# A two-block float32 forward pass: three products of the mixing and ple phases summed in one set of 256 PSUM columns

## The chip, the cores and the metric

One core of a Trainium2 chip runs the whole program. The metric is the device time of one execution in microseconds (us). Engines are called as the profile calls them: PE is TensorE, DVE VectorE, ACT ScalarE, POOL GpSimd and SP SyncE, whose queue issues the weight loads from HBM.

## What is computed

Two transformer-like blocks on one sequence of 256 positions with 2048 channels, all in float32. Each block projects its input, runs small mixers on the projections (a linear recurrence, pooling, short convolution and attention in the first; two kinds of attention in the second), sums their gated projections, and then runs a feed-forward part. The lines that matter here are the gated sums and the small product `e`:

```python
# first block: four branches of width 512
branches = jnp.einsum('bskw,kwd->bskd', ys, w_branch[l])
merged = jnp.sum(gates * branches, axis=2)
x = x + merged @ w_out[l]
# second block: two branches of width 512, and e from p of width 256
mix = (gate_a * ya + gate_b * yb) @ w_out[i]       # ya, yb: branch outputs @ w_branch_a, w_branch_b
e = p[i] @ w_ple_in[i]
h = h + jax.nn.sigmoid(h @ w_ple_gate[i]) * e
```

## The kernel before

Everything is kept transposed: 128 channels on the partitions, 256 positions (`S`) along the free dimension. Every large product runs as a stream of **units**. A unit makes 256 output channels (two tiles `t` of 128) by 256 positions. Its weights come in **pieces** of 512 KB: four k-tiles of 128 rows by 256 columns (two k-tiles in the phase `ple`). A phase (`plan()`, lines 120 to 158) is a list of units with one source of weights; most have 4 pieces in a unit (`ppu`), the four phases `mix_a0` to `mix_a3`, the two phases `mix_b0` and `mix_b1` and the phase `ple` have one. Each of these seven phases has 8 units.

To hold float32 accuracy, each operand is split into a high part (rounded to the format `fp32r`) and a low part (the rest). For activations, high and low stand side by side, 512 columns (`act_a`, `act_b`); for weights they are two buffers, `wh` and `wl`. A piece passes through a ring of four slots:

- SP loads it into `raw` (line 547) when DVE has split the piece four earlier.
- ACT makes `wh` (line 879) when the load has landed and PE has used the piece four earlier (`w_used`).
- DVE makes `wl = raw - wh` (line 1216).
- PE runs, for each k-tile and each t, two matmuls (lines 580 and 582): `wh` by the 512 columns [high | low], and `wl` by the 256 columns of high. So PSUM holds in columns 0:256 the sum wh·xh + wl·xh, and in columns 256:512 the sum wh·xl. A unit takes one of two PSUM buffers in turn, and a new unit waits until the unit two earlier has been summed (`summed`).

The **epilogue** of a unit adds the two halves: ACT copies columns 256:512 to `bcopy` (line 893), and DVE adds columns 0:256 to it (line 1241, or 1236 for `ple`, `w_out2` and `ffn_down0`). In the mixing phases a unit is one branch of one pair of output tiles. DVE multiplies its sum by the gate (line 1288 for the first branch, 1290 for the others), and POOL adds the later branches to the merged sum (line 1675). In `mix_a3` and `mix_b1` the finished sum also has to be split for the next phase: POOL's addition, then ACT's high part (line 932), then DVE's low part (line 1225).

Each engine runs its instructions strictly in the written order. In the mixing phases the order is that of `threaded`: DVE and ACT hold three pieces of lead (piece u+3 is prepared between the epilogue steps of unit u). At the end of such a phase the first pieces of the next phase (3 if it is a mixing phase, 4 otherwise) are prepared after the epilogue of unit 6 and ahead of that of unit 7. `ple` runs in the order of `fed` with one piece of lead, and its last units are interleaved with the normalisation before `ffn_up0` (`post_norm`, line 1605 on DVE).

## Time and profile before

| | us |
|---|---|
| median of 3 runs | 3088.48 (3086.43 to 3089.05) |
| the profiled execution, its own time | 3071.16 |
| its span, first to last instruction | 3069.3 |
| mean granted TensorE clock | 0.988 |

The span is what the rows below describe. Sections of the profile: busy time of each engine, the span in slices, the DMA queues, the chain that ended last, and groups of instructions by source line. Other views used are stretches of the span with the busy time of each engine, and timelines of one engine, in which a bracket gives the idle time ahead of an instruction and what ended it. Instructions of one engine overlap a little at their edges, so the distance of two starts is often less than the duration of the first.

### The profile page before, as it was taken

How to read it: one execution, taken by the hardware profiler on the slowest of the kernel's cores; microseconds unless marked ns; L12 is line 12 of the kernel's file. 1: busy time of each engine (PE TensorE's matmuls, PEld its weight loads, DVE VectorE, ACT ScalarE, POOL GpSimd, SP SyncE). 2: the span in 40 equal slices, each digit the busy share in tenths (PEclk: the TensorE clock that was granted, in tenths of full speed). 3: DMA queues.
4: the chain of work that ended last, by engine and by line, in shares of the span. 5: the costliest groups of instructions: out<-in, count | busy, mean ns of one | idle time of the engine just before them, and what ended most of it. 6: DMA issues, size and time to landing. Idle time of an engine off the chain costs nothing. (4 is left out here: it accounts for less than half of the span.)

```text
span 3069.3 us, 48743 instructions
## 1 busy us (share of the span) xinstructions
PE 2967.5 (97%) x16830; PEld 2571.2 (84%) x16830; DVE 1973.4 (64%) x2245; ACT 1551.1 (51%) x1953; POOL 257.8 (8%) x217
## 2 busy tenths in 40 slices
PE   7999999999999999999999998999799999999979
PEld 6788888888888888888888887878588888888867
DVE  6486676656665656556656655665777567657664
ACT  5485654454544444444544455444466455545544
POOL 3010011102101010000200000001300000010131
PEclk9999999999999999999999999999899999999989
DMA  7555557665666666665665544546366666565545
GB/s 215 158 165 165 165 167 217 181 178 171 192 192 192 189 188 191 190 187 180 197 191 172 170 148 141 185 151 190 107 187 185 186 190 189 187 185 185 173 134 165
DMA packets 544861, 544.78 MB, mean 177 GB/s; under 512 B 17032, under 2 KB 543880, under 8 KB 544752
## 3 DMA queue, kind: packets, MB, share of 16 engines
q1 hardware_dynamic: 543200, 539.42, 57.7%
q0 software_dynamic: 1552, 3.97, 0.4%
q8 instruction: 60, 0.98, 0.1%
q14 instruction: 49, 0.40, 0.0%
HBM read 541.23 MB, written 2.10 MB: 177 GB/s over the span
## 5 line engine op out<-in xcount | busy, mean ns | idle before, releaser
L1216 DVE TENSOR_TENSOR w_low<-raw,w_high 128x1024 fp32r<-128x1024 f32 x1024 | 1276.3, 1260 | 857.1 <-ACT w_high L879 852.6
L580 PE MATMUL ps_gemm<-act_a,w_high 128*128 128x512 f32 x4640 | 1643.1, 399 | 60.5 <-DVE w_low L1216 39.2
L879 ACT CAST w_high<-raw 128x1024 fp32r<-128x1024 f32 x1024 | 1056.6, 1045 | 961.7 <-PE ps_gemm L582 925.4
L582 PE MATMUL ps_gemm<-act_a,w_low 128*128 128x256 f32 x4640 | 1303.8, 281 | 0.0
L580 PE MATMUL ps_gemm<-act_b,w_high 128*128 128x512 f32 x3520 | 1240.6, 397 | 14.9 <-DVE w_low L1216 5.7
L580 PEld LDWEIGHTS ps_gemm<-act_a,w_high 128*128 128x128 f32 x4640 | 876.9, 189 | 276.6 <-issue 59.5
L582 PE MATMUL ps_gemm<-act_b,w_low 128*128 128x256 f32 x3520 | 986.9, 280 | 0.0
L582 PEld LDWEIGHTS ps_gemm<-act_a,w_low 128*128 128x128 f32 x4640 | 882.6, 190 | 0.2
L580 PEld LDWEIGHTS ps_gemm<-act_b,w_high 128*128 128x128 f32 x3520 | 663.3, 188 | 170.6 <-issue 10.6
L582 PEld LDWEIGHTS ps_gemm<-act_b,w_low 128*128 128x128 f32 x3520 | 667.8, 190 | 0.2
L893 ACT COPY bcopy<-ps_gemm 128x512 f32<-128x512 f32 x300 | 173.6, 579 | 88.1 <-PE ps_gemm L582 88.0
L1241 DVE TENSOR_TENSOR summ<-ps_gemm,bcopy 128x512 f32<-128x512 f32 x276 | 188.8, 684 | 28.1 <-ACT bcopy L893 27.3
L1689 POOL TENSOR_TENSOR proj<-proj,summ 128x512 f32 x32 | 41.4, 1292 | 1016.3 <-DVE summ L1241 1016.3
L1304 DVE SCALAR_TENSOR_TENSOR gates<-summ,params,gates 128x254 f32<-128x254 f32 (+1 forms) x176 | 77.3, 480 | 17.7 <-ACT gates L946 10.7
L1250 DVE TENSOR_TENSOR summ<-summ,rstd 128x512 f32<-128x512 f32 x124 | 85.8, 692 | 4.3
L1675 POOL TENSOR_TENSOR proj<-proj,summ 128x512 f32 x32 | 46.5, 1455 | 400.2 <-DVE summ L1290 400.2
L1657 POOL TENSOR_TENSOR sqacc<-sqacc,sqt 128x512 f32<-128x512 f32 x48 | 67.8, 1413 | 126.4 <-ACT sqt L964 114.3
L912 ACT CAST act_a<-summ 128x512 f32 (+1 forms) x32 | 19.9, 622 | 96.9 <-DVE summ L1263 96.9
L946 ACT ACTIVATE gates<-summ,params 128x256 f32<-128x256 f32 x88 | 48.2, 595 | 21.0 <-DVE summ L1250 19.0
L1257 DVE SCALAR_TENSOR_TENSOR act_b<-proj,params,act_b (+1 forms) x32 | 26.6, 873 | 49.8 <-ACT act_b L905 49.8
L899 ACT ACTIVATE gates<-summ 128x512 f32<-128x512 f32 (+1 forms) x40 | 25.3, 632 | 63.1 <-DVE summ L1250 63.0
L1225 DVE TENSOR_TENSOR act_a<-summ,act_a 128x512 f32 (+1 forms) x32 | 22.2, 693 | 32.5 <-ACT act_a L912 32.5
(239 smaller groups left out, 911.0 us busy)
## 6 DMA issues: line engine op xcount, KB each, us to landing
raw<-in_w_in SPq DMA_DIRECT2D x352, 512.0 KB, 4.2
raw<-in_w_up SPq DMA_DIRECT2D x176, 512.0 KB, 3.6
raw<-in_w_mlp_up SPq DMA_DIRECT2D x128, 512.0 KB, 3.9
raw<-in_w_mlp_down SPq DMA_DIRECT2D x128, 512.0 KB, 4.2
raw<-in_w_down SPq DMA_DIRECT2D x88, 512.0 KB, 4.4
raw<-in_w_out SPq DMA_DIRECT2D x64, 512.0 KB, 4.6
raw<-in_w_branch SPq DMA_DIRECT2D x32, 512.0 KB, 4.0
raw<-in_w_ple_gate SPq DMA_DIRECT2D x32, 512.0 KB, 4.4
```

The source lines that it names most:

```text
L580: nc.tensor.matmul(ps[:, g, t, :], wh[:, at, o:o + P], x, start=first, stop=False, skip_group_check=True)
L582: last = nc.tensor.matmul(ps[:, g, t, 0:S], wl[:, at, o:o + P], high(x), start=False, stop=final, skip_group_check=True)
L879: nc.scalar.copy(wh[:, at, 0:kn * S], raw[:, at, 0:kn * S]).then_inc(high_ready, 1)
L893: nc.scalar.copy(bcopy[:, g], ps[:, g, :, S:2 * S]).then_inc(b_copied, 1)
L946: last = nc.scalar.activation(G[:, 28 + 2 * j + t, :], summ[:, g, t], ACT.Identity, scale=pcol("conv_w2", c0 + t + 176), bias=pcol("conv_b ...
L1216: nc.vector.tensor_tensor(wl[:, at, 0:kn * S], raw[:, at, 0:kn * S], wh[:, at, 0:kn * S].bitcast(F32), ALU.subtract).then_inc(split_done, 1)
L1241: nc.vector.tensor_tensor(s2, A_half, bcopy[:, g], ALU.add).then_inc(summed, 1)
L1250: nc.vector.tensor_tensor(s2, s2, r2, ALU.mult).then_inc(scaled, 1)
L1304: last = nc.vector.scalar_tensor_tensor(out=y[:, t, sh:S], in0=summ[:, g, t, 0:S - sh], scalar=pcol("conv_w2", c0 + t + 88 * tap), in1=y[: ...
L1657: nc.gpsimd.tensor_tensor(sqacc[:], sqacc[:], sqt[:, g], ALU.add).then_inc(inc, 1)
L1675: nc.gpsimd.tensor_tensor(d, d, s2, ALU.add).then_inc(merged if split else epi_done, 1)
L1689: nc.gpsimd.tensor_tensor(d, d, s2, ALU.add).then_inc(epi_done, 1)
```

## The change

In the phases `mix_a0` to `mix_a3`, `mix_b0`, `mix_b1` and `ple` (the function `folded`), the 512-column matmul becomes two of 256 columns, `wh` by high and `wh` by low, and both go to PSUM columns 0:256, where `wl` by high goes too. PSUM then holds the full sum, and columns 256:512 are no longer used. ACT's epilogue returns at once (no copy). DVE waits for PE itself (`w_used`): in the mixing phases it multiplies PSUM by the gate in one instruction, in `ple` it copies PSUM to its place. For a first branch DVE now waits for the end of that multiplication and for the unit before, and then signals `epi_done` by hand. POOL waits for `summed` in place of `scaled`. Counters are adjusted for the units that have no copy. Of `ADDS`, the entries of the branch phases under `scaled` go. `source`, `over`, `threaded` and `fed` are unchanged.

```diff
@@ -113,6
+def folded(ph):
+    return ph.kind.startswith("branch") or ph.name == "ple"
...
+        copied += 0 if folded(x) else x.units
...
+def copied_no(ph, i, j):
+    return i * ph.U + (ph.copied0 + j)
...
@@ -577,8 +587,14 @@
                     final = s == ph.ppu - 1 and k == kn - 1
                     for t in range(2):
                         o = k * S + t * P
-                        nc.tensor.matmul(ps[:, g, t, :], wh[:, at, o:o + P], x,
-                                         start=first, stop=False, skip_group_check=True)
+                        if folded(ph):
+                            nc.tensor.matmul(ps[:, g, t, 0:S], wh[:, at, o:o + P], high(x),
+                                             start=first, stop=False, skip_group_check=True)
+                            nc.tensor.matmul(ps[:, g, t, 0:S], wh[:, at, o:o + P], x[:, S:2 * S],
+                                             start=False, stop=False, skip_group_check=True)
+                        else:
+                            nc.tensor.matmul(ps[:, g, t, :], wh[:, at, o:o + P], x,
+                                             start=first, stop=False, skip_group_check=True)
                         last = nc.tensor.matmul(ps[:, g, t, 0:S], wl[:, at, o:o + P], high(x),
                                                 start=False, stop=final, skip_group_check=True)
                 last.then_inc(w_used, 1)
@@ -888,6 +904,8 @@
 
             def epilogue(ph, i, j):
                 k, g, n = ph.kind, bank(ph, j), unit_no(ph, i, j)
+                if folded(ph):
+                    return
                 act.wait_ge(w_used, end_piece(ph, i, j))
                 act.wait_ge(summed, n + 1)
                 nc.scalar.copy(bcopy[:, g], ps[:, g, :, S:2 * S]).then_inc(b_copied, 1)
@@ -1229,10 +1247,19 @@
                 t0 = dst_tile(ph, i, j)
                 A_half = ps[:, g, :, 0:S]
                 s2 = summ[:, g]
-                dve.wait_ge(b_copied, n + 1)
+                if folded(ph):
+                    dve.wait_ge(w_used, end_piece(ph, i, j))
+                else:
+                    dve.wait_ge(b_copied, copied_no(ph, i, j) + 1)
                 dve.wait_ge(epi_done, n + 1)
+                if ph.name == "ple":
+                    nc.vector.tensor_copy(tiles(G, t0, 2), A_half).then_inc(summed, 1)
+                    dve.wait_ge(summed, n + 1 + 2)
+                    dve.wait_ge(epi_done, n + 2)
+                    dve.sem_inc(epi_done, 1)
+                    return
                 if k in ("mix", "store"):
-                    dst = tiles(G, t0, 2) if ph.name == "ple" else tiles(PJ, t0 + 16, 2)
+                    dst = tiles(PJ, t0 + 16, 2)
                     nc.vector.tensor_tensor(dst, A_half, bcopy[:, g], ALU.add).then_inc(summed, 1)
                     dve.wait_ge(summed, n + 1 + 2)
                     dve.wait_ge(epi_done, n + 2)
@@ -1281,13 +1308,17 @@
                 def gated():
                     nb = 4 if k.startswith("branch4") else 2
                     br = j % nb
+                    dve.wait_ge(w_used, end_piece(ph, i, j))
+                    dve.wait_ge(epi_done, n + 1)
+                    total = ps[:, g, :, 0:S]
                     gate = gate_tiles(ph, i * 2 + 4 * br) if nb == 4 else tiles(G, i * 4 + (12 + 8 * br + 2 * (j // 2)), 2)
-                    dve.wait_ge(summed, n + 1 + 2)
                     if br == 0:
+                        nc.vector.tensor_tensor(tiles(PJ, t0 + 16, 2), total, gate, ALU.mult).then_inc(summed, 1)
+                        dve.wait_ge(summed, n + 1 + 2)
                         dve.wait_ge(epi_done, n + 2)
-                        nc.vector.tensor_tensor(tiles(PJ, t0 + 16, 2), s2, gate, ALU.mult).then_inc(epi_done, 1)
+                        dve.sem_inc(epi_done, 1)
                     else:
-                        nc.vector.tensor_tensor(s2, s2, gate, ALU.mult).then_inc(scaled, 1)
+                        nc.vector.tensor_tensor(s2, total, gate, ALU.mult).then_inc(summed, 1)
                         if br == nb - 1 and k.endswith("s"):
                             dve.wait_ge(high_out, after("high_out", ph, i, j))
                             low(tiles(act_a if nb == 4 else act_b, t0, 2), tiles(PJ, t0 + 16, 2), epi_done)
@@ -1324,7 +1355,7 @@
                         low(tiles(act_b, t0, 2), G[:, 30:32, :], epi_done)
                 if k == "upconv":
                     return [total, taps, product, rest]
-                return [total, gated] if k.startswith("branch") else [total]
+                return [gated] if k.startswith("branch") else [total]
 
             def recip(n):
 
@@ -1667,7 +1698,7 @@
                 if k.startswith("branch"):
                     nb = 4 if k.startswith("branch4") else 2
                     if j % nb:
-                        pool.wait_ge(scaled, after("scaled", ph, i, j))
+                        pool.wait_ge(summed, n + 1 + 2)
                         pool.wait_ge(epi_done, n + 2)
                         d = tiles(PJ, t0 + 16, 2)
                         split = j % nb == nb - 1 and k.endswith("s")
```

## Rows read from the trace of the kernel before

**Rows 1.** Page, part 1: busy time of each engine, share of span, instructions.
```profile
PE 2967.5 (97%) x16830; PEld 2571.2 (84%) x16830; DVE 1973.4 (64%) x2245; ACT 1551.1 (51%) x1953; POOL 257.8 (8%) x217
```

**Rows 2.** Stretches mix_a0, mix_b1: length; busy PE, PEld, DVE, ACT, POOL; clock; DMA.
```profile
430.00:456.20 26.20, 25.02 (x140) 21.08 (x138) 23.64 (x25) 13.02 (x18) 7.18 (x5) 1.00 0.51 159
2044.00:2073.00 29.00, 22.66 (x110) 18.97 (x109) 21.22 (x27) 12.08 (x18) 3.86 (x3) 0.88 0.41 126
```

**Rows 3.** PE's timeline at full pace in mix_a0: start, duration, instruction.
```profile
437.86 0.40 PE L580 MATMUL ps_gemm<-act_b,w_high 128*128 128x512 f32 x1
438.10 0.28 PE L582 MATMUL ps_gemm<-act_b,w_low 128*128 128x256 f32 x1
438.21 0.40 PE L580 MATMUL ps_gemm<-act_b,w_high 128*128 128x512 f32 x1
...
439.98 0.40 PE L580 MATMUL ps_gemm<-act_b,w_high 128*128 128x512 f32 x1
```

**Rows 4.** PE's timeline at full pace in mlp_up0, the same columns.
```profile
849.81 0.39 PE L580 MATMUL ps_gemm<-act_b,w_high 128*128 128x512 f32 x1
...
851.89 0.39 PE L580 MATMUL ps_gemm<-act_b,w_high 128*128 128x512 f32 x1
```

**Rows 5.** PE's timeline: 18 transposes, each with its own weight load.
```profile
1723.28 2.17 PE L794 MATMUL ps_small<-proj 128*128 128x128 f32 x18
```

**Rows 6.** Groups by line: busy us, mean ns | idle before, releaser.
```profile
L582 PEld LDWEIGHTS ps_gemm<-act_b,w_low 128*128 128x128 f32 x3520 | 667.8, 190 | 0.2
L893 ACT COPY bcopy<-ps_gemm 128x512 f32<-128x512 f32 x300 | 173.6, 579 | 88.1 <-PE ps_gemm L582 88.0
L1675 POOL TENSOR_TENSOR proj<-proj,summ 128x512 f32 x32 | 46.5, 1455 | 400.2 <-DVE summ L1290 400.2
```

**Rows 7.** DVE's timeline in mix_a0 and at its end.
```profile
441.58 0.68 DVE L1241 TENSOR_TENSOR summ<-ps_gemm,bcopy 128x512 f32<-128x512 f32 x1
442.18 2.11 DVE L1216 TENSOR_TENSOR w_low<-raw,w_high 128x1024 fp32r<-128x1024 f32 x1
444.22 0.68 DVE L1290 TENSOR_TENSOR summ<-summ,gates 128x512 f32<-128x512 f32 x1
444.82 0.68 DVE L1241 TENSOR_TENSOR summ<-ps_gemm,bcopy 128x512 f32<-128x512 f32 x1
...
450.36 1.32 DVE L1290 TENSOR_TENSOR summ<-summ,gates 128x512 f32<-128x512 f32 x1
451.60 4.58 DVE L1216 TENSOR_TENSOR w_low<-raw,w_high 128x1024 fp32r<-128x1024 f32 x3
456.10 0.68 DVE L1241 TENSOR_TENSOR summ<-ps_gemm,bcopy 128x512 f32<-128x512 f32 x1
```

**Rows 8.** PE's timeline: stops at the edges of mix_a0 and mix_a2, in mix_a3, after mix_b0.
```profile
452.87 0.50 PE L580 MATMUL ps_gemm<-act_b,w_high 128*128 128x512 f32 x1 [0.93 <-DVE w_low L1216]
456.90 0.49 PE L580 MATMUL ps_gemm<-act_b,w_high 128*128 128x512 f32 x1 [0.96 <-DVE summ L1241]
592.32 0.50 PE L580 MATMUL ps_gemm<-act_a,w_high 128*128 128x512 f32 x1 [0.94 <-DVE w_low L1216]
704.37 0.49 PE L580 MATMUL ps_gemm<-act_b,w_high 128*128 128x512 f32 x1 [2.10 <-DVE summ L1241]
710.95 0.50 PE L580 MATMUL ps_gemm<-act_a,w_high 128*128 128x512 f32 x1 [0.76 <-DVE w_low L1216]
1945.30 0.50 PE L580 MATMUL ps_gemm<-act_b,w_high 128*128 128x512 f32 x1 [1.21 <-DVE w_low L1216]
```

**Rows 9.** DVE's timeline in mix_b1: the first and the last low part.
```profile
2049.34 0.69 DVE L1225 TENSOR_TENSOR act_b<-proj,act_b 128x512 fp32r<-128x512 f32 x1 [2.41 <-ACT act_b L932]
...
2075.24 0.69 DVE L1225 TENSOR_TENSOR act_b<-proj,act_b 128x512 fp32r<-128x512 f32 x1 [2.41 <-ACT act_b L932]
```

**Rows 10.** DVE's timeline in ple: two of its sums.
```profile
2167.34 0.69 DVE L1236 TENSOR_TENSOR gates<-ps_gemm,bcopy 128x512 f32<-128x512 f32 x1 [2.19 <-ACT bcopy L893]
...
2185.48 0.69 DVE L1236 TENSOR_TENSOR gates<-ps_gemm,bcopy 128x512 f32<-128x512 f32 x1 [0.64 <-ACT bcopy L893]
```

More of the change, by code:

```diff
@@ L98, in __init__ @@
         self.quarter, self.group, self.half = quarter, group, half
-        self.piece0 = self.unit0 = self.bodies = 0
+        self.piece0 = self.unit0 = self.bodies = self.copied0 = 0
         self.count0 = {}
 ADDS = {
-    "scaled": {"gate": [1, 1, 1, 1], "branch4": [0, 1, 1, 1], "branch4s": [0, 1, 1, 1], "branch2": [0, 1, 0, 1],
-               "branch2s": [0, 1, 0, 1], "up": [1, 1], "upconv": [1, 1], "final": [1, 1]},
+    "scaled": {"gate": [1, 1, 1, 1], "up": [1, 1], "upconv": [1, 1], "final": [1, 1]},
     "acted": {"up": [1, 1], "upconv": [1, 1], "final": [1, 1]},
@@ L147, in plan @@
     ph.append(Phase("final", 8, 2, 4, name="ple_gate"))
-    piece = unit = 0
+    piece = unit = copied = 0
     count = {k: 0 for k in ADDS}
@@ L151, in plan @@
         assert x.units % x.U == 0 and (x.U % 2 == 0 or x.units == 1) and (x.U * x.ppu) % RING == 0
-        x.piece0, x.unit0, x.bodies = piece, unit, x.units // x.U
+        x.piece0, x.unit0, x.bodies, x.copied0 = piece, unit, x.units // x.U, copied
         x.count0 = dict(count)
```

## The prediction

> **What bounds the kernel now.** I read part 1 of the page first. PE is busy for 97% of the span [rows 1], so for most of the run an instruction taken from ACT or DVE is worth nothing. Next I read the stretches of the phases that the change touches, for here PE does stop. In `mix_a0` it is busy 25.02 of 26.2 us, and DVE 23.64. In `mix_b1` PE is busy 22.66 of 29.0 us, and the clock that it was granted falls to 0.88 [rows 2]. Last I read the timelines, to see who ends the stops.
>
> At full pace one pair (512 and 256 columns) takes (439.98 - 437.86) / 6 = 0.353 us [rows 3]. A mixing unit has 8 pairs, 2.83 us. DVE in the same unit does a sum, a weight split and a gate: from 441.58 to 444.82 is 3.24 us [rows 7]. So in the mixing phases DVE is slower than PE by 0.41 us a unit. Its split takes 2.11 us here, against a mean of 1.53 for the three that start at 451.60. The difference is POOL's addition beside it, 1.46 us on average [rows 6, 7]. The three pieces of lead hide this inside a phase. It shows at the edges: PE stops before the first unit of the next phase, which waits for DVE's split, and before the second, which waits for DVE's sum of the old phase's last unit [rows 8]. That sum stands behind three splits, at 456.10 [rows 7].
>
> **What the change does to PE.** Each of the 6 x 64 mixing pairs gets one matmul and one weight load more, with the same number of columns. The trace has no two 256-column matmuls of this format in a row. The nearest row is the 256-column one between two others: its successor starts 0.11 us later (438.10 to 438.21), and in that time a full weight load was taken in [rows 3]. Three such steps are 0.33 to 0.35 us, against the pair's 0.353 now. Can loads follow at this rate? In 18 transposes in a row, each with a load of 128x128, the starts are (2.17 - 0.28) / 17 = 0.11 us apart [rows 5]. I therefore take the pair as unchanged. The bounds: three times 0.11 gains 0.02 us x 384 = 8 us; a load that can't be hidden costs 66 us (below).
>
> The Trainium skill, TensorE: Matmul & The Clock Gate, section LDWEIGHTS, gives a load as its columns divided by 1.2, 107 ns for 128; by that, three loads would fit the pair, and rows 3 and 5 agree. The Trainium skill, Perfetto Trace Analysis, Identifying the Most-Contended Engine, speaks against the change: it judges TensorE by the busy share of LDWEIGHTS. That share is 21.08 of 26.2 us in mix_a0 [rows 2], and with half as many loads again it would be 120%.
>
> **What it does to ACT.** 48 copies of 0.58 us go from the mixing phases and 8 from ple [rows 6]. ACT's busy time there is about half the stretch [rows 2], so the 32 us of work are worth nothing by themselves. What counts is that DVE no longer waits for the copy, and that casts no longer stand behind it. DMA issues hang on DVE's splits alone and move forward with them; no queue is blocked more than now.
>
> **What it does to DVE.** In a mixing unit two instructions of 0.68 us (0.60 from start to start, 444.22 to 444.82) become one [rows 7]. I price it at 0.68 too, since it reads one operand from PSUM and one from SBUF, as the sum does. A unit then takes 3.24 - 0.60 = 2.64 us, 0.19 less than PE. Added: a first-branch unit waits for its own end, priced at 0 to 0.25 us. Behind it on DVE stands the next split, which has three pieces of lead. One more thing helps: the gate that reads two SBUF tiles took 1.32 us beside POOL at 450.36; the sum from PSUM at 441.58 did not stretch [rows 7].
>
> The gains, edge by edge. A bracket's idle time understates a stop: the matmul ahead is drawn 0.28 us long, but its successor could start after 0.11, and the first matmul after a stop is 0.10 longer [rows 3, 8]. I add 0.26 to each.
>
> - mix_a0 to mix_a1: 0.93 and 0.96 idle, and the like of the first at the end of mix_a1: 3 x 1.2 = 3.6 us [rows 8]. After the change unit 6 is done on DVE 0.68 + 2.11 = 2.8 us after PE ends it, split of the next piece included, and PE's unit 7 takes 2.83. I leave 0.1 of each stop: gain 3.3.
> - mix_a2: 0.94 idle, gain 1.1 [rows 8].
> - mix_a3: 2.10 and 0.76 idle, 3.4 with the additions [rows 8]. The 2.10 come from the detour POOL, ACT, DVE (2.41 idle on DVE in its twin in mix_b1 [rows 9]). DVE reaches the detour one unit's wait earlier, as it is no longer late: gain 3.3. The stop ahead of the phase's third unit, where DVE is busy with the merged low parts, stays.
> - mix_b0: 1.21 idle, gain 1.5 [rows 8].
> - mix_b1: here four detours in eight units make DVE's own chain the bound, up to the last low part at 2075.24 [rows 9], on which the next phase's third piece waits. Each of 8 units loses one instruction, 0.60; after three detours only about 0.47 counts, as DVE then waits for ACT's cast. That is 4.4 us. The own-end waits of four first branches give back 0.25 each at most: 3.4 to 4.4, I take 4.0.
> - ple: DVE copies instead of summing, at the same 0.68. Only the waits for ACT shrink: 0.64 of the idle at 2185.48 and one copy's time, 0.58, at 2167.34 [rows 6, 10], and 0.58 more where ACT's cast no longer stands behind a copy: 1.8. What is late next is DVE in `post_norm`, unchanged.
>
> Sum: 3.3 + 1.1 + 3.3 + 1.5 + 4.0 + 1.8 = 15.0, and 1 of the 8 us that PE's pair could gain at best: 16 us. Against the profiled execution, 3071.2 - 16 = 3055 us; that execution is 17.3 us under the median, and I take the same gain from the median: 3088.5 - 16 = 3072.5 us.
>
> **The rivals.** *The weight load becomes PE's bound.* If loads don't overlap each other, a pair needs 3 x 0.190 = 0.57 us [rows 6], a unit 4.56 instead of 2.83: 48 x 1.73 = 83 us more, less the stops, which vanish: about 3155 us. It decides as soon as a load and a 256-column matmul need over 0.118 us. For it: the loads' share in rows 2, and that no three short steps in a row are in the trace. Against it: rows 5. In a mild form (10 ns for each added matmul) it costs 4 us and leaves 3076.
>
> *DVE stays the bound.* The margin of 0.19 us a unit is thin: if a wait or POOL's port takes 0.2 to 0.3 us a unit, the edges keep half their stops. Gain 16 - 1/2 x (3.3 + 1.1 + 3.3 + 1.5) = 11, less 1 to 2 in mix_b1: 3079 us.
>
> *PE's pace changes with the form or the code's place.* The same pair takes 0.347 us in mlp_up0 (2.08 / 6) [rows 4] and 0.353 in mix_a0, and the rows don't say why. If two 256-column matmuls beat the 512-column one, the lower bound above holds: 3065 us. If a later phase of 256 pairs passes from one pace to the other, that is 1.7 us either way for each.
>
> *The gain is given back later,* because the chain through `post_norm` or the loads holds the end: the phases behind are bound by PE, which starts them earlier, so I see no place for it. Time within 0.2%.
>
> **How the numbers follow.** Forecast 3072.5: 0.58. DVE stays the bound, 3079: 0.15. A faster pair, 3065: 0.12. Given back or nothing gained: 0.06. The load as a bound: 0.09. The range takes in the forecast with its errors, the faster pair and the half gain, and leaves out the last two: 3063 to 3082. A measurement of this kernel can tell about 0.2%, 6 us, from no change. Faster by more: 0.84; within: 0.07; slower: 0.09.
>
> **What would show it.** In the changed kernel's trace the pair of rows 3 becomes three starts about 0.115 us apart; three at 0.15 or more refute the first step. DVE's cycle in mix_a0 falls from 3.24 us to PE's 2.83, with idle time ahead of the gate that PE ends. The stops of rows 8 are under 0.3 us, apart from the kept one. The four low parts of mix_b1 span 22 us instead of 25.9 [rows 9]. In ple the sums wait for PE. Wrong would be: a PE that is busy throughout mix_a0 with a longer stretch (loads), or the stops of rows 8 unchanged (DVE).

## The result and the profile after

| | before | after |
|---|---|---|
| median (range) of 6 runs each, one comparison | 3088.8 (3086.4 to 3101.7) us | 3061.4 (3055.6 to 3068.3) us |
| profiled execution (its span) | 3071.2 (3069.3) us | 3064.2 (3062.4) us |
| all runs of this study: number, median, mean with its error | 85, 3077.2, 3077.8 ± 0.9 us | 23, 3060.9, 3062.7 ± 1.4 us |

The ratio of the first comparison is 0.9913 [0.989, 0.9936]: 27 us less, where I had forecast 16, and 3061.4 lies below the range (3063 to 3082). But the two profiled executions differ by only 6.9 us in span, and over all runs of the study the medians differ by 16.3 us, the means by 15.1. So there are three figures for one change, and the explanation must give all three. Below, a gain given beside a ratio is worked out from the ratio.

The page of after, part 1, and the groups that answer to [rows 1] and [rows 6]:

```profile
PE 2972.5 (97%) x17246; PEld 2590.4 (85%) x17246; DVE 1933.2 (63%) x2197; ACT 1523.7 (50%) x1897; POOL 265.4 (9%) x217
```
```profile
L911 ACT COPY bcopy<-ps_gemm 128x512 f32<-128x512 f32 x244 | 140.9, 577 | 35.7 <-PE ps_gemm L598 35.7
...
L1706 POOL TENSOR_TENSOR proj<-proj,summ 128x512 f32 x32 | 55.5, 1733 | 378.0 <-DVE summ L1321 377.9
...
L591 PE MATMUL ps_gemm<-act_b,w_high 128*128 128x256 f32 x256 | 72.7, 284 | 2.5 <-DVE proj L1316 2.3
```

PE has 416 matmuls more: 384 in the mixing phases and 32 in ple, which my count of the pairs had left out. ACT's copies fell from 300 to 244, DVE has 48 instructions fewer, and one thing rose that I had not looked at: POOL's addition, from 1455 to 1733 ns.

The stretches mix_a0 and mix_b1 of after (length; busy PE, PEld, DVE, ACT, POOL; clock; DMA), against [rows 2]:

```profile
433.50:457.00 23.50, 23.50 (x198) 23.50 (x197) 15.46 (x16) 9.88 (x10) 9.38 (x5) 1.00 0.51 161
2031.00:2064.00 33.00, 28.81 (x221) 27.35 (x220) 22.22 (x31) 14.59 (x23) 4.55 (x4) 1.00 0.45 134
```

The stretch of mix_a0 ends here ahead of the stop at the phase's edge, and that of [rows 2] behind it. The stretch of before that leaves the edge out in the same way is this one:

```profile
429.20:451.80 22.60, 22.60 (x128) 19.30 (x127) 19.38 (x22) 12.27 (x17) 5.16 (x4) 1.00 0.54 170
```

Inside the phase PE is busy throughout in both kernels, and DVE's share fell from 86% to 66%; what became of the edge is shown below. In mix_b1 PE still stops, but the granted clock is 1.00 over the whole stretch, not 0.88.

PE's timeline in mix_a0 of after, against [rows 3]:

```profile
436.94 0.28 PE L591 MATMUL ps_gemm<-act_b,w_high 128*128 128x256 f32 x1
437.06 0.28 PE L593 MATMUL ps_gemm<-act_b,w_high 128*128 128x256 f32 x1
437.18 0.28 PE L598 MATMUL ps_gemm<-act_b,w_low 128*128 128x256 f32 x1
437.30 0.28 PE L591 MATMUL ps_gemm<-act_b,w_high 128*128 128x256 f32 x1
```

Three steps of 0.12 make 0.36 us, where the pair took 0.353 or 0.347. Now DVE's and POOL's timelines in mix_a0 of after, against [rows 7], and last POOL's in before beside the split of 442.18:

```profile
442.90 0.69 DVE L1321 TENSOR_TENSOR summ<-ps_gemm,gates 128x512 f32<-128x512 f32 x1 [1.06 <-PE ps_gemm L598]
443.51 1.22 DVE L1234 TENSOR_TENSOR w_low<-raw,w_high 128x1024 fp32r<-128x1024 f32 x1
445.78 0.69 DVE L1316 TENSOR_TENSOR proj<-ps_gemm,gates 128x512 f32<-128x512 f32 x1 [1.06 <-PE ps_gemm L598]
```
```profile
443.80 2.07 POOL L1706 TENSOR_TENSOR proj<-proj,summ 128x512 f32 x1 [0.81 <-DVE summ L1321]
```
```profile
441.93 1.28 POOL L1675 TENSOR_TENSOR proj<-proj,summ 128x512 f32 x1 [1.95 <-DVE summ L1290]
```

The cycle is 445.78 - 442.90 = 2.88 us, which is PE's eight triples (8 x 0.36). DVE waits 1.06 us of it for PE. The split takes 1.22 us, not 2.11, and this time it is POOL's addition that is long. It begins at 443.80, behind the split's begin at 443.51. In before it began at 441.93, ahead of the split at 442.18, took 1.28 us, and the split was the long one. The order changed because POOL is released by the gate: in before a sum of 0.60 us stood between the gate and the split, and in after the split follows the gate at once. The Trainium skill, SBUF — State Buffer, SBUF: two separate sides, has VectorE with two SBUF inputs and GpSimd share one pair of ports, which whoever starts first keeps for its whole instruction; the two traces agree (2.11 us in one order, 2.07 on POOL in the other). Nobody waits for POOL here, so the exchange is free.

The stops of PE in after, against [rows 8], the first at the edge to mix_a1, the second the kept one in mix_a3, the others in mix_b1:

```profile
457.46 0.38 PE L591 MATMUL ps_gemm<-act_b,w_high 128*128 128x256 f32 x1 [0.20 <-DVE summ L1321]
...
689.84 0.38 PE L591 MATMUL ps_gemm<-act_b,w_high 128*128 128x256 f32 x1 [2.27 <-DVE proj L1316]
...
2037.71 0.39 PE L591 MATMUL ps_gemm<-act_a,w_high 128*128 128x256 f32 x1 [0.92 <-DVE proj L1316]
...
2044.55 0.38 PE L591 MATMUL ps_gemm<-act_a,w_high 128*128 128x256 f32 x1 [0.83 <-DVE proj L1316]
...
2051.39 0.38 PE L591 MATMUL ps_gemm<-act_a,w_high 128*128 128x256 f32 x1 [0.82 <-DVE proj L1316]
```

And DVE in mix_b1 of after, its first and last low part and the wait for its own end, against [rows 9]:

```profile
2041.99 0.69 DVE L1243 TENSOR_TENSOR act_b<-proj,act_b 128x512 fp32r<-128x512 f32 x1 [2.40 <-ACT act_b L950]
2044.60 1.23 DVE L1234 TENSOR_TENSOR w_low<-raw,w_high 128x1024 fp32r<-128x1024 f32 x1 [0.18 <-DVEq L1319]
...
2065.37 0.69 DVE L1243 TENSOR_TENSOR act_b<-proj,act_b 128x512 fp32r<-128x512 f32 x1 [2.39 <-ACT act_b L950]
```

The four low parts span 23.38 us (25.90 before, 22 forecast), and the detour over ACT (2.40) is untouched.

### The profile page after: what moved, and what is told of

Its sections match the earlier page's. It is cut to its first block and busy times, and to the rows that moved or that the text cites. A ratio compares the mean times of both kernels' runs of the same rounds, so it can differ in the third digit from the quotient of the medians.

```text
span 3062.4 us, 49424 instructions
## 1 busy us (share of the span) xinstructions
PE 2972.5 (97%) x17246; PEld 2590.4 (85%) x17246; DVE 1933.2 (63%) x2197; ACT 1523.7 (50%) x1897; POOL 265.4 (9%) x217
## 5 line engine op out<-in xcount | busy, mean ns | idle before, releaser
L596 PE MATMUL ps_gemm<-act_a,w_high 128*128 128x512 f32 x4480 | 1584.8, 399 | 43.7 <-DVE w_low L1234 25.8
L596 PE MATMUL ps_gemm<-act_b,w_high 128*128 128x512 f32 x3264 | 1150.2, 398 | 6.3 <-DVE act_b L1243 4.7
L596 PEld LDWEIGHTS ps_gemm<-act_a,w_high 128*128 128x128 f32 x4480 | 846.4, 189 | 252.0 <-issue 41.4
L596 PEld LDWEIGHTS ps_gemm<-act_b,w_high 128*128 128x128 f32 x3264 | 614.2, 188 | 153.6 <-issue 6.0
L1268 DVE TENSOR_TENSOR summ<-ps_gemm,bcopy 128x512 f32<-128x512 f32 x228 | 156.0, 684 | 22.0 <-ACT bcopy L911 21.4
L911 ACT COPY bcopy<-ps_gemm 128x512 f32<-128x512 f32 x244 | 140.9, 577 | 35.7 <-PE ps_gemm L598 35.7
L1720 POOL TENSOR_TENSOR proj<-proj,summ 128x512 f32 x32 | 41.4, 1293 | 1016.2 <-DVE summ L1268 1016.2
L1706 POOL TENSOR_TENSOR proj<-proj,summ 128x512 f32 x32 | 55.5, 1733 | 378.0 <-DVE summ L1321 377.9
L591 PE MATMUL ps_gemm<-act_b,w_high 128*128 128x256 f32 x256 | 72.7, 284 | 2.5 <-DVE proj L1316 2.3
L593 PE MATMUL ps_gemm<-act_b,w_high 128*128 128x256 f32 x256 | 72.4, 283 | 0.0
L591 PE MATMUL ps_gemm<-act_a,w_high 128*128 128x256 f32 x160 | 48.4, 302 | 10.6 <-DVE w_low L1234 8.0
```

Of the source, the lines that this page charges most:

```text
L591: nc.tensor.matmul(ps[:, g, t, 0:S], wh[:, at, o:o + P], high(x), start=first, stop=False, skip_group_check=True)
L593: nc.tensor.matmul(ps[:, g, t, 0:S], wh[:, at, o:o + P], x[:, S:2 * S], start=False, stop=False, skip_group_check=True)
L596: nc.tensor.matmul(ps[:, g, t, :], wh[:, at, o:o + P], x, start=first, stop=False, skip_group_check=True)
L911: nc.scalar.copy(bcopy[:, g], ps[:, g, :, S:2 * S]).then_inc(b_copied, 1)
L1268: nc.vector.tensor_tensor(s2, A_half, bcopy[:, g], ALU.add).then_inc(summed, 1)
L1706: nc.gpsimd.tensor_tensor(d, d, s2, ALU.add).then_inc(merged if split else epi_done, 1)
```

## How the spans were taken apart

From the starts of the matmuls of a trace I took two sums. *Stops*: what a start-to-start time has beyond the step usual there (0.116 us behind 256 columns, 0.233 behind 512), waits and stretches at the lower clock alike, where it is over 0.13 or 0.25. *Pace*: for every 512 + 256 pair that ran unbroken, what it took beyond 0.3467 us, the shorter of the two paces of [rows 3, 4]. The rest is span less both. How the small matmuls between the phases are counted moves the sum of stops as a whole: over all matmuls it is 142.7 us in before and 124.4 in after, over those of the large products alone 196.2 and 177.8. The difference stays 18.3 or 18.4, and only differences are used here.

| execution | span | stops | pace | rest |
|---|---|---|---|---|
| before | 3069.3 | 192.3 | 19.3 | 2857.7 |
| before again (e1_before) | 3084.9 | 192.6 | 34.6 | 2857.7 |
| after | 3062.4 | 174.0 | 25.0 | 2863.4 |
| after again (e2_after) | 3059.1 | 173.7 | 22.1 | 2863.3 |
| after, third (e12_after5) | 3064.4 | 174.6 | 25.7 | 2864.1 |

The stops fell by 18.5 us, alike in every execution. The rest rose by about 6 us: these are the 416 triples, which are counted in no pace (416 x (0.360 - 0.3467) = 5.5 us). And the pace has nothing to do with the change: it differs by 15 us between two executions of the very same kernel, which is their difference in span (15.6). The experiments below take these three apart.

## Experiments

**The kernel before, again.** No edit, three rounds.

> The kernel before, once more, for a second profile. Between the first two profiles the spans differ by 6.9 us, the medians of the runs by 27 us. Theory A (pace): whole phases run at 0.347 or 0.353 us a pair of matmuls, and which one is drawn anew in each execution; then this profile has the same PE stops as the first (within 1 us in all phases together), but other phases at the slow pace, and its span lies by up to 20 us above 3069.3, 1.7 us for each phase of 256 pairs that changed. Theory B (stops): the executions differ in PE stops; then a longer span comes with more stop time and the paces are as before. The time is that of the kernel before, ratio 1.000 within 0.002.

Measured: 3073.1 us (3064.1 to 3088.2) against 3074.5 of its partner, ratio 1.000 [0.9979, 1.0022]. The first comparison's 3088.5 is at the upper end of what this kernel shows. Its profiled execution was 15.6 us longer than the first one of before, and almost all of it lies in one stretch, from the first pair behind the row sums of mlp_up0 to the row sums behind the last mlp phase. PE's timeline, first of before, then of before again:

```profile
813.91 0.59 PE L580 MATMUL ps_gemm<-act_b,w_high 128*128 128x512 f32 x1
...
1524.08 0.59 PE L615 MATMUL ps_small<-sqacc,common 128*128 128x256 f32 x2
```
```profile
815.71 0.58 PE L580 MATMUL ps_gemm<-act_b,w_high 128*128 128x512 f32 x1
...
849.81 0.40 PE L580 MATMUL ps_gemm<-act_b,w_high 128*128 128x512 f32 x1
...
851.93 0.40 PE L580 MATMUL ps_gemm<-act_b,w_high 128*128 128x512 f32 x1
...
1539.52 0.59 PE L615 MATMUL ps_small<-sqacc,common 128*128 128x256 f32 x2
```

The same work, without a stop in either, takes 710.17 us in one and 723.81 in the other. [Rows 4] have six pairs in 2.08 us (0.347 each); here the same six, at the same place of the program, take 2.12 (0.353). So the pace doesn't belong to a line or a form: the same instructions have one or the other.

**The kernel after, again.** No edit.

> The changed kernel, once more, for a second profile. Theory A: the PE stops in the changed phases are as in its first profile (about 20 us fewer than before in all), the folded group of three matmuls takes 0.360 us in every mixing phase again, and the span differs from 3062.4 only by phases at the other pace. Theory B: the stops differ. Ratio to the kernel before 0.991 within 0.003.

Measured: 3060.8 us (3054.5 to 3077.3), ratio 0.996 [0.9937, 0.9983], a gain of 12 us. Five rounds more (e12_after5) gave 3063.4 us (3050.9 to 3076.6), 0.9939 [0.9907, 0.9971], a gain of 19. The 27 us of the first comparison did not come back.

> The changed kernel against the kernel before in more rounds, as the draws of the pace spread single runs over 25 us. So far the ratios are 0.991 and 0.996. By the profiles' parts: PE stops 192.4 - 173.9 = 18.6 us fewer; 384 groups at 0.360 against a mean of 0.350 us cost 3.8; so about 15 us less, a ratio of 0.9952, within 0.002. If the first comparison's 27 us were real, 0.991.

**Only the split of the matmul.** In before, the 512-column matmul of the mixing phases and ple as two of 256, into the columns as of old; copy and sum stay.

```diff
-nc.tensor.matmul(ps[:, g, t, :], wh[...], x, start=first, ...)
+nc.tensor.matmul(ps[:, g, t, 0:S], wh[...], high(x), start=first, ...)
+nc.tensor.matmul(ps[:, g, t, S:2 * S], wh[...], x[:, S:2 * S], start=False, ...)
...
```

> The matmul alone: in the mixing phases and ple the 512-column matmul is two of 256 columns, but into the old columns, and ACT's copy and DVE's sum stay. Stops theory: the three matmuls take 0.360 us against 0.353, so PE needs 2.88 us a unit, and DVE's cycle of 3.24 us still bounds the mixing phases; most of the 0.06 us a unit is hidden, and the time is 0 to 3 us above the kernel before. Weight-load rival of the prediction in its mild form: 4 us or more above. If the gain of the change came from the form of the matmuls or from the place of the code, this kernel would be faster than before by 5 us or more.

Measured: 3076.3 us, ratio 1.0015 [0.9998, 1.0033]: +4.6 us, inside its noise (its mean is 0.5 ± 2.6 us above that of all runs of before). Its stops sum to 187.6 us, 5 less than before's, though nothing was taken from DVE. DVE's timeline shows why:

```profile
446.77 0.68 DVE L1247 TENSOR_TENSOR summ<-ps_gemm,bcopy 128x512 f32<-128x512 f32 x1
447.40 2.07 DVE L1222 TENSOR_TENSOR w_low<-raw,w_high 128x1024 fp32r<-128x1024 f32 x1
...
450.00 0.68 DVE L1247 TENSOR_TENSOR summ<-ps_gemm,bcopy 128x512 f32<-128x512 f32 x1
```

DVE's cycle is 3.23 us as before, and PE's is 2.88 instead of 2.8. PE catches up with DVE more slowly and stops for less. So a slower PE gives its own price back, as shorter stops: by the traces 4.7 us of stops against the 4 to 5.5 us that 416 triples cost.

**The split in every phase,** to see the price of the form by itself.

```diff
-if ph.kind.startswith("branch") or ph.name == "ple":
+if True:
```

> The kernel before with the 512-column matmul made two of 256 columns, into the same columns as before, in every phase. This prices the form alone on some 8000 groups, where PE is the bound. If three matmuls always take 0.360 us, as in the mixing phases of the changed kernel, against a pair that is drawn at 0.347 or 0.353: 8000 x 0.010 = 80 us more, at most 8160 x 0.0133 = 109, so a median of 3140 to 3175. If the 0.360 belongs to short phases only and the three also have a faster pace of 3 x 0.1167 = 0.350: 0 to 30 us more. If a load were the bound: several hundred us more.

Measured: 3156.0 us (3153.6 to 3158.6), ratio 1.0245 [1.0198, 1.0293]. Against the 3077.2 of all runs of before that is 78.8 us on 24990 - 16830 = 8160 triples, 0.0097 us each. PE's timeline and part 1 of its page:

```profile
1000.00 0.28 PE L581 MATMUL ps_gemm<-act_a,w_high 128*128 128x256 f32 x1
1000.12 0.28 PE L583 MATMUL ps_gemm<-act_a,w_high 128*128 128x256 f32 x1
1000.24 0.28 PE L588 MATMUL ps_gemm<-act_a,w_low 128*128 128x256 f32 x1
1000.36 0.28 PE L581 MATMUL ps_gemm<-act_a,w_high 128*128 128x256 f32 x1
```
```profile
PE 3057.0 (97%) x24990; PEld 3026.7 (96%) x24990; DVE 1968.9 (62%) x2245; ACT 1549.9 (49%) x1953; POOL 257.9 (8%) x217
```

The steps are 0.120 again. There is no fast variant of the triple: its four runs lie within 5 us, where the ten of before in e1_before spread over 24. Four runs are few, but that is what one expects if the two paces exist only for the pair. For the change it means 416 x 0.0097 = 4.0 us of cost.

The Trainium skill, Perfetto Trace Analysis, Identifying the Most-Contended Engine, asks for the busy share of LDWEIGHTS (beside the share of the peak rate that the matmuls reach). It went to 100% in mix_a0 of after and to 96% here, and the time did rise, so the page pointed the right way; the size it could not tell, since these records overlap (0.19 us long, 0.12 apart).

**DVE keeps its second instruction.** In after, DVE copies the sum from PSUM and then gates it; ACT's copy stays out.

```diff
+def copied():
+    dve.wait_ge(w_used, end_piece(ph, i, j))
+    ...
+    nc.vector.tensor_copy(s2, ps[:, g, :, 0:S]).then_inc(summed, 1)
 def gated():
-    total = ps[:, g, :, 0:S]
+    total = s2
...
-return [gated] if k.startswith("branch") else [total]
+return [copied, gated] if k.startswith("branch") else [total]
```

> The changed kernel, but in the mixing phases DVE keeps two instructions: it copies PSUM to summ and then multiplies by the gate. ACT's copy is gone and the three products are folded. If DVE's instruction is what the gain comes from: DVE's cycle in mix_a0 is again about 3.2 us, the stops at the ends of the mixing phases return, and of some 27 us only 4 to 8 us remain (ple, and DVE's waits for ACT's copy in mix_a3 and mix_b1). If the removed ACT copy is what counts: 20 us or more remain.

Measured: 3070.8 us, ratio 0.9984 [0.9964, 1.0004], a gain of 4.9 us. DVE's timeline in its mix_a0, and the stop of PE at the phase's end:

```profile
441.59 0.69 DVE L1312 COPY summ<-ps_gemm 128x512 f32<-128x512 f32 x1
442.20 2.08 DVE L1235 TENSOR_TENSOR w_low<-raw,w_high 128x1024 fp32r<-128x1024 f32 x1
444.20 0.68 DVE L1324 TENSOR_TENSOR summ<-summ,gates 128x512 f32<-128x512 f32 x1
444.80 0.68 DVE L1312 COPY summ<-ps_gemm 128x512 f32<-128x512 f32 x1
...
456.89 0.38 PE L592 MATMUL ps_gemm<-act_b,w_high 128*128 128x256 f32 x1 [0.91 <-DVE summ L1312]
```

The cycle is back at 3.21 us, the split back at 2.08, and the stop is back. The stops sum to 185.9 us: of the 18.5 that the change saves, 6.4 are left. Not all of these 6.4 belong to ACT's copy, for PE's slower triples alone bring the sum from 192.3 to 187.6. Set in a row, the traces give:

| step | stops, whole span | stops at the edges of the folded phases |
|---|---|---|
| before | 192.3, 192.6 | 44.2, 43.5 |
| triples alone (e3_split_only) | 187.6 | 39.9 |
| products folded, ACT's copy out too (e7_dve_two) | 185.9 | 35.5 |
| one DVE instruction less too (after) | 174.0, 173.7, 174.6 | 24.6, 26.4, 26.3 |

The last column adds up the stops from mix_a0 to w_out and from mix_b0 to ple, over the matmuls of the large products. It leaves out some 3 us of stops that e7_dve_two has elsewhere, in phases that are the same in all four kernels. So the DVE instruction carries 10 to 12 us of the 18, the slower PE 4 to 5, and ACT's copy 2 to 4. The long split beside POOL comes back with the instruction (0.60 us for the one, up to 0.86 for the other, in a unit); the two come and go together here, and no run separates them. In the timed runs e7_dve_two's mean is 10.2 ± 2.9 us above after's, which agrees.

**ACT keeps a copy.** In after, a copy of the old size from SBUF to SBUF on ACT behind each folded unit, for which nobody waits.

```diff
 if folded(ph):
+    act.wait_ge(w_used, end_piece(ph, i, j))
+    act.wait_ge(summed, n + 1)
+    ...
+    nc.scalar.copy(extra[:], common[:, 0:252]...).then_inc(act_chain, 1)
     return
```

> The changed kernel with ACT's copy put back at its old place in the folded phases, after PE has ended the unit (SBUF to SBUF, 504 columns in place of 512), with nobody waiting for it; ACT's next cast stands behind it. If ACT's work matters only where DVE waits for it: the PE stops of mix_a0 to mix_a2 and mix_b0 stay near those of the changed kernel, mix_b1 and ple lose 1 to 2 us together, and the time is 0 to 3 us above the changed kernel. If the removed ACT work were half of the gain: 6 to 10 us above.

Measured: 3069.8 us (3057.0 to 3081.6), ratio 0.9976 [0.9949, 1.0003]. Its stops sum to 176.3 us, 2 above after's. ACT's, DVE's and PE's timelines at the end of its mix_a0 show where they come from:

```profile
450.42 2.94 ACT L896 CAST w_high<-raw 128x1024 fp32r<-128x1024 f32 x3
...
451.50 2.66 DVE L1242 TENSOR_TENSOR w_low<-raw,w_high 128x1024 fp32r<-128x1024 f32 x2 [1.06 <-ACT w_high L896]
...
453.09 0.38 PE L592 MATMUL ps_gemm<-act_b,w_high 128*128 128x256 f32 x1 [0.50 <-DVE w_low L1242]
```

The next phase's casts stand behind the copy (and behind its wait), DVE waits 1.06 us for one of them, and PE 0.50. By its stops ACT's copy is worth about 2 us (3 to 4 at the edges alone), as casts that stand behind it, and not as ACT's 32 us of work. The expectation had them in the wrong place: mix_b1 lost nothing (3.4 us of stops, as in after), and the edges of mix_a0 to mix_a2 went from 0.5 us to 2.5. The timed runs don't bear the small size out: their mean is 7.8 ± 3.0 us above after's, which lies in the rival's 6 to 10 and doesn't rule out the 3 of the expectation's end. The one profiled execution is among the faster of the ten, and its pace is that of after, so its trace can't say where the other 4 to 5 us would lie. The worth of ACT's copy is therefore 2 to 4 us by the traces and open by the times.

**The merged parts spread out.** A version that might beat both. The stops left in mix_a3 and mix_b1 come where ACT and DVE make the merged operand's high and low parts in one go. Here a few of them are made behind each unit: two a unit in mix_a3, three behind every other one in mix_b1.

```diff
-for t in range(n):
-    dve.wait_ge(m_high, first + t + 1)
-    low(buf[:, t:t + 1, :], PJ[:, 16 + t:17 + t, :], m_low)
+def low_t(t):
+    dve.wait_ge(m_high, first + t + 1)
+    low(buf[:, t:t + 1, :], PJ[:, 16 + t:17 + t, :], m_low)
+return [lambda t=t: low_t(t) for t in range(n)]
...
+some(ph, j)       # behind the unit's gate, and in ACT's epilogue
```

> The changed kernel with the 12 (mix_a3) and 8 (mix_b1) high and low parts of the earlier merged tiles made a few at a time beside the units, 2 a unit in mix_a3 and 3 in DVE's wait of the detour in mix_b1, instead of all at once ahead of the first gate. The kept stop of 2.6 us ahead of the third unit and the slow clock behind it should go: PE stops of mix_a3 from about 3.4 us (2.6 and 4.2 in the two profiles) to under 1, of mix_b1 from 6.8 to 3 to 5. In all 4 to 7 us faster than the changed kernel. Rival: DVE has no room, its chain in mix_b1 grows by the lows: 0 to 2 us.

Measured: 3060.6 us, 0.9952 [0.9931, 0.9972]; with five rounds (e13_spread5) 3058.8 us (3052.3 to 3068.2), 0.9923 [0.9895, 0.9952].

> The kernel with the spread merged parts, again, beside the changed kernel on the same chip. Its profile had 170.6 us of PE stops against 173.9: 3 us less than the changed kernel, ratio to the kernel before 0.9942 within 0.002. Rival: no difference that can be told.

The mean of its 17 runs is 3060.3 ± 1.2 us, 17.5 under before's and 2.4 under after's. The last difference is little more than its error (1.8), and under the 4 to 7 us forecast. The first profile (e10_spread) has 170.6 us of stops, 3.4 under after's. The second (e13_spread5) has 176.3, more than after's: 5.6 us more than the first, all of it in gates_a0, gates_a1 and gates_b0, which the edit doesn't touch. In both profiles the stops in mix_a3 are 1.3 us where after has 2.6 to 4.2, those in mix_b1 with the start of the next phase 5.3 where after has 6.8. PE's stop moved from the third unit of mix_a3 to a later one and is half as long, and in mix_b1 DVE makes spread parts early (2041.75) and waits 0.48 us for ACT ahead of a low part, where in after it waits 2.40. PE's and DVE's timelines of e10_spread:

```profile
700.12 0.38 PE L599 MATMUL ps_gemm<-act_b,w_high 128*128 128x256 f32 x1 [1.06 <-DVE proj L1327]
...
2041.75 2.18 DVE L1254 TENSOR_TENSOR act_b<-proj,act_b 128x256 fp32r<-128x256 f32 x3
2044.42 0.69 DVE L1254 TENSOR_TENSOR act_b<-proj,act_b 128x512 fp32r<-128x512 f32 x1 [0.48 <-ACT act_b L959]
```

**Breaks in the long stretch.** If PE's pace is drawn whenever its stream of pairs is broken, and kept until the next break, then breaks put into the stretch from 814 to 1524 us should make a mixture of paces out of one. In before, two small matmuls ahead of seven of the mlp phases; their result is used by nobody.

```diff
+def redraw():
+    ...
+    nc.tensor.matmul(pm[:, 3, 0:S], ones, common[:], start=True, stop=False)
+    nc.tensor.matmul(pm[:, 3, 0:S], ones, common[:], start=False, stop=True)
 for g in range(4):
...
+        redraw()
         units(BY[f"mlp_up{g}"], from_buf(act_b))
+    redraw()
     units(BY[f"mlp_down{g}"], from_buf(act_a), after_phase(f"mlp_up{g}"))
```

> The kernel before with two small float32 matmuls (2 x 2 records of 0.215 us) ahead of each phase from mlp_down0 to mlp_down3, seven places where PE now runs on without a break. Theory: the pace, 0.347 or 0.353 us a pair, is drawn where PE's stream is broken and kept until the next break. Then the stretch of 710 us from mlp_up0 to mlp_down3, at one pace in every profile so far, shows both paces in one profile, changing at the new matmuls alone; the time is 7 x 0.9 = 6 us above the kernel before plus or minus the draws, and the spread of the runs (3064 to 3088, 14 us of it from this stretch) is smaller. Rival: the pace belongs to the phase or the execution; then the stretch stays at one pace.

Measured: 3085.5 us, ratio 1.0032 [1.0008, 1.0055]. The eight segments between the breaks ran fast, slow, fast, fast, slow, fast, fast, slow. PE's timeline across the first break:

```profile
889.97 0.40 PE L580 MATMUL ps_gemm<-act_b,w_high 128*128 128x512 f32 x1
...
892.05 0.40 PE L580 MATMUL ps_gemm<-act_b,w_high 128*128 128x512 f32 x1
...
892.40 0.59 PE L743 MATMUL ps_small<-common 128*128 128x256 f32 x2
892.83 0.59 PE L744 MATMUL ps_small<-common 128*128 128x256 f32 x2
...
893.61 0.40 PE L580 MATMUL ps_gemm<-act_a,w_high 128*128 128x512 f32 x1
...
895.73 0.40 PE L580 MATMUL ps_gemm<-act_a,w_high 128*128 128x512 f32 x1
```

Six pairs take 2.08 us ahead of the break and 2.12 behind it, 0.347 and 0.353 each. In the ten other traces with pairs the whole stretch has one pace: fast in seven, slow in three. And no unbroken run of 20 pairs or more, 548 of them in these eleven traces, changes its pace inside. The breaks cost 7 x 0.87 = 6.1 us of stops by its trace (198.5 in all), which answers to the +10 us. The spread did not become clearly smaller: nine of its ten runs lie between 3081.3 and 3091.7, one at 3103.5. That was the weaker half of the test, and ten runs don't settle it.

The three sums close the account for these kernels too:

| execution | span | stops | pace | rest |
|---|---|---|---|---|
| e3_split_only | 3066.8 | 187.6 | 14.7 | 2864.5 |
| e7_dve_two | 3081.8 | 185.9 | 33.2 | 2862.7 |
| e8_act_extra | 3062.8 | 176.3 | 23.2 | 2863.3 |
| e10_spread | 3054.5 | 170.6 | 20.7 | 2863.2 |
| e13_spread5 | 3055.1 | 176.3 | 15.4 | 2863.4 |
| e11_redraw | 3082.8 | 198.5 | 25.7 | 2858.6 |

The rest is 2857.7 to 2858.6 us in the three executions without triples and 2862.7 to 2864.5 in the eight with 416 of them, whatever DVE and ACT do. The spans by themselves would mislead: e7_dve_two's is 19 us above after's, and 8 of these are pace.

Folding only some of the phases, which would show each phase's share in the timed difference by itself, was not tried on the chip.

## Why the prediction was right or wrong

**The base was wrong, and the size came out right by luck.** I had forecast a gain of 16 us and took it from the median of three executions, 3088.5. Over all 85 runs of before the median is 3077.2; 16 from that is 3061.2, and after's 23 runs have 3060.9. The step that failed is "I take the same gain from the median": the median of three, 3088.5, was 11 us above what this kernel takes over 85 runs, and the range stood on it. The size, 16 against 15.1 ± 1.7 between the means (14 ± 2 without the first comparison), is two errors that nearly cancel: the stops were put 3.5 us too low, and the form of the matmuls at +1 where it costs 4. I had noted that the profiled execution was 17.3 us under the median, and [rows 3, 4] showed two paces of one pair. Their difference, 0.0067 us, times the 7744 pairs that the change leaves alone is 52 us at the most, and 13.6 us were seen in one stretch. The rival on the pace had it as a matter of form or place and priced it at 1.7 us for a phase. It is a matter of the execution, and one draw can hold for eight phases. That makes the range too narrow for a comparison of six runs. That the timed runs of the first comparison had slow paces in before is argued, not shown: timed runs leave no trace. What speaks for it is that the profiled executions of all kernels differ in pace by 20 us (14.7 to 34.6) and the timed runs of before by about 25 apart from outliers. What speaks against it as the whole cause: all six runs of before in the first comparison took 3086.4 us or more, and only 9 of the 79 later ones did. Six draws that know nothing of each other would hardly all fall there. Either the paces of one occasion hang together, or something else held before back in that comparison and not after, whose six runs (median 3061.4) agree with its later ones; no run settles it.

**PE's form.** Forecast a gain of 1 us; it costs 4. I read 0.11 us as the step of a 256-column matmul behind a load, but [rows 3] have only its one step between two others, which are 0.24. Three short ones in a row take 0.120 each. That the load behind the short one had the long neighbour's time to hide in is my reading; no run separates the load from the matmul. The rival in its mild form, 10 ns for each added matmul and 4 us in all, is what came. Its strong form (0.57 us a triple) and the fast one (0.33) didn't.

**The stops.** Forecast 15.0 us; measured 18.5. By place, before to after, each in all executions of the two kernels:

| edge | forecast gain | measured |
|---|---|---|
| mix_a0, mix_a1 | 3.3 | 4.0 to 0.6: 3.4 |
| mix_a2 | 1.1 | 1.3 to 0: 1.3 |
| mix_a3 | 3.3 | 7.7 or 8.1 to 2.6 or 4.2: 3.5 to 5.5 |
| mix_b0 | 1.5 | 1.7 to 0: 1.7 |
| mix_b1 and the start behind | 4.0 | 12.3 to 6.8: 5.5 |
| ple to ffn_up0 | 1.8 | 34.8, 35.5 to 32.4, 34.2, 34.0: 1.6 between the means |

Right ahead of mix_b0, in gates_b0, both executions of before and one of the three of after have a stretch at the lower clock too, worth 1.5 us; it lies ahead of the folded phase, and I don't count it as the change's.

The waits alone came as priced, or a little less in mix_b1: DVE's chain there lost 2.5 us over three periods, where I had 3.9. What I had not priced was PE's clock behind a stop. Stretches of before in mix_b1, then of after and of after again in mix_a3 (columns as in [rows 2]):

```profile
2051.00:2054.00 3.00, 3.00 (x11) 2.58 (x11) 3.00 (x4) 1.17 (x2) 0.00 (x0) 0.54 0.26 71
...
2068.00:2071.00 3.00, 2.85 (x9) 2.47 (x10) 3.00 (x4) 1.57 (x3) 0.00 (x0) 0.55 0.51 152
```
```profile
692.00:698.00 6.00, 6.00 (x53) 6.00 (x52) 3.62 (x4) 1.05 (x1) 5.20 (x3) 1.00 0.75 215
```
```profile
692.00:698.00 6.00, 6.00 (x43) 6.00 (x42) 3.18 (x4) 1.05 (x1) 3.87 (x2) 0.78 0.72 213
```

In mix_b1 of before (the first fence) the granted clock was 0.54, near the lower level, 1.2 GHz (0.50), behind the stops of 2.4 and 3.9 us, and 11 and 9 matmuls ran in 3 us, where at 0.353 a pair 17 would. In after no stop there is longer than 1.9 us, and the clock is 1.00. In mix_a3 the kept stop of 2.5 us is followed by 1.00 in after, as shown, and by 0.78 in the same place of after again: this too differs by execution, and is the 1.6 us between 2.6 and 4.2.

**DVE.** Right: its cycle fell under PE's, it waits for PE in the units inside a phase, and e7_dve_two shows that its instruction, with the split that shortens with it, carries half to two thirds of the saved stops. The rival "DVE stays the bound" failed because the margin was larger than the 0.19 us I gave it: with no sum between gate and split, the split starts ahead of POOL's addition and takes 1.22 us, not 2.11. I had used the long one. The margin is 1.06 us.

**ACT.** Right in kind by the traces: the copy's 32 us are worth 2 to 4 us of stops, as casts that stand behind it. By the timed runs of e8_act_extra its worth is open.

**Own end waits.** Priced at 0 to 0.25 us each; 0.18 (the row at 2044.60).

**The sum.** 18.5 of stops less 4.0 of form is 14.5 us; the means of all runs differ by 15.1 ± 1.7.

## What to carry to other kernels

Before a forecast is set against a median, look whether executions of the unchanged kernel differ, and in what: compare the start-to-start time of one repeated pair at several places and in two traces. A change of half a per cent needs some twenty runs of each kernel here, taken in several comparisons; six of each in one gave 27 us for a change worth 15. And price a matmul's step from a row in which its neighbours are like it: a 256-column one between 512-column ones showed 0.11 us here, and 0.120 among its like.

A slower stream on the bound engine isn't paid in full where that engine also stops for another; taking one short instruction from the engine it stops for saved more stops here (10 to 12 us) than taking all 32 us of copies from a third one (2 to 4).

## What the runs showed of the hardware

- A pair of 512 and 256 columns has two paces, 0.347 and 0.353 us. One is taken up when the stream is broken, by a stop or by other matmuls, and held to the next break, for 2048 pairs if there is none (710.17 or 723.81 us). Which one comes differs between executions of one kernel at the same place, but not at every place: the 255 to 310 pairs that start near 480 us are slow in all eleven traces. What decides is open.
- Three matmuls of 256 columns, each with its load, take 0.120 us each at a granted clock of 1.00, in every mixing phase of after's three traces and in the long phases of e9_split_all. The first few behind a stop or behind a pair can be nearer (0.117), and in ple, which stops often, the mean is 0.119.
- The stretched partner in a meeting of DVE's two-input instruction with POOL's addition changes with their order: DVE 2.11 us or POOL 2.07.
- The granted clock was 0.54 and 0.55 in stretches of before right behind stops of 2.4 and 3.9 us in mix_b1, and 1.00 behind stops of up to 1.9 us in the same phase of after; behind one of 2.5 us it was 1.00 in one execution and 0.78 in another.
